# A transposed key block in the pipeline of a hybrid encoder layer: where it is transposed and copied, and how the last loads are cut

## The chip, the cores and the metric

The kernel runs on one core of a Trainium2 chip. The metric is the device time of one execution in microseconds; the median of three runs is given. A core has TensorE (PE, with its weight loads PEld), VectorE (DVE), ScalarE (ACT), GpSimd (POOL) and SyncE (SP, which here only issues DMAs). Every engine works through its own instructions in order and waits for the others by semaphores.

## What is computed

One layer over 2048 tokens of width 1024, all in float32. The reference, cut to what matters here:

```
u = rms_norm(x)
z = u @ w_in + b_in                     # q_a k_a v_a g_a lr_a | q_b k_b v_b
b = cumsum(log_sigmoid(lr_a @ w_a2 + b_a2) / 16)   # inside chunks of 64 tokens
q_dec = q_a * exp(b) / 8 ; k_inv = k_a * exp(-b) ; k_end = k_a * exp(b_last - b)
o_a = tril(q_dec @ k_inv.T) @ v_a + q_dec @ S      # gated linear attention, 4 heads
S   = exp(b_last) * S + k_end.T @ v_a              # its state, once per chunk
o_b = softmax(q_b @ k_b.T / 8 - alibi, sink) @ v_b # window of 128 tokens, 8 heads
x = x + concat(norm(o_a) * silu(g_a), o_b) @ w_out
x = x + MoE(rms_norm(x))                # 32 experts, 2 per token
y = rms_norm(x)
```

The change concerns k_end (in the code `keT`, features by tokens, and `ke`, tokens by features) and the loads of the last norm.

## The kernel before

The 2048 tokens are 16 tiles of 128. The first half of the time is the mixer: a software pipeline of steps i = 0 to 17, written by `pipeline` as two steps, a loop of seven pairs, and two steps. Step i projects tile i (`new` work), finishes attention and output of tile i-1 (`old`), and routes tile i-2 (`old2`). One function per engine (`pe_iter`, `act_iter`, `dve_iter`, `pool_iter`, `sp_iter`) writes out that engine's order by hand. Then come the routing tables, a loop over the 32 experts, and the final norm (`finish`).

`JOBS` (L91) lists what TensorE writes into PSUM in a step; entry k uses bank k mod 8, with the lag of its tile behind the step and the semaphore that tells that its result was taken. `bank_free` goes back eight entries at a time to the last job that ran in the same bank and gives the semaphore to wait for. An entry named spare is never computed and only keeps a place.

TensorE's order in step i: `qk` (queries and keys of the linear attention, transposed, 64 matmuls, L299 in the trace), `keT` (two transposes of tile i-1's decayed keys, L288), `u2Ta` and `u2Tb` (transposes of h, L288), `att` (L350), `dS` (the state's increment from `ke` and v, L361), `v` (L293), router (L376), transposes of the softmax's probabilities (L288), `g` (L293), `og`, `ob`, `kv`, `mixAT`, `qb` with the low-rank gate `la` inside (L455), a matmul for the next x (L306), `wo` in two halves (output projection, L321), and the scores `s0` to `s3` (L470).

VectorE at the end of step i: the cumulative sum and differences of the gate, `spread_x` (L642, eight products that make the next uT, for which `qk` of step i+1 waits), the first half of the routing choice (`choose`, L600 to L608), the first half of h (L780, needs the first half of `wo`), the second half of the choice (L610 to L622), the second half of h (L780), the gate's log sigmoid (L783), the three products with the decays, which make `qdkiT` and `keT` (L788, L790, L792), then the scores out of PSUM (L800, four), their maximum (L807 to L812). Step i+1 begins with the wait for the exponentials' sums, the scaling of the probabilities (L671), the bias of `qk` (L680) and `u2T` (L686, for which the router's matmuls wait).

ScalarE at the end of step i: the gates' exponentials and logarithms (L542 to L558), the three decays (L562 to L564, semaphore `decays_ready`), dec (L566), the square of h (L570, needs both halves of h), the sigmoid's exponential (L573, needs L783), eight softmax exponentials (L576) and the sink's (L577). Step i+1 then begins with the copy of the transposed keys from PSUM to `ke` (L493), for which `dS` waits.

In the final norm (`finish`) SP issues loads of h from DRAM in the pieces of `PIECES` (L1313), four loads of 1, 3, 6 and 6 tiles, and then the 16 stores of the output (L1343). ScalarE squares tile by tile (L1362), waiting for a piece at its first tile; GpSimd makes the roots in groups of three tiles (L1346, L1348), and VectorE scales (L1369). ScalarE's squares of tiles 4 on stand in its order behind two squares of the last expert's sums (L1388).

Of the kernel before, what the change touches and what calls it, by code (L numbers as in the profile page):

```python
# [75 lines left out]
class Semaphores:  # L76
# [12 lines left out]


JOBS = [  # L91
    ("qk", 0, {"qk_ready": (1, 1)}), ("keT", 1, {"ke_ready": (1, 1)}),
    ("u2Ta", 2, {"u2T_ready": (2, 1)}), ("u2Tb", 2, {"u2T_ready": (2, 2)}),
    ("att0", 1, {"att_ready": (2, 1)}), ("att1", 1, {"att_ready": (2, 2)}),
    ("dS0", 1, {"Smid_ready": (1, 1)}),
# [13 lines left out]
]  # L109
CHOOSE_STEPS = 18  # L110
INDEX = {name: k for k, (name, _, _) in enumerate(JOBS)}
# [2 lines left out]
def mixer(nc, sem, bank, A, C, scratch, ctx):  # L114
# [160 lines left out]
    def pe_iter(pe, i, par):  # L275
# [52 lines left out]
        if on("qk"):  # L328
# [3 lines left out]
            for n in range(4):  # L332
                m = project_T("qk", C_QK + n * P, C_QK + (n + 1) * P, n * P)
            m.then_inc(sem("qk_done"), 1)
        if on("keT"):
            wait(pe, sem("keT_ready"), i)
            transposes("keT", lambda c: keT[:, c * P:(c + 1) * P], 2)
        for n, name in enumerate(("u2Ta", "u2Tb")):
            if on(name):
                wait(pe, sem("h_ready"), 2 * (i - 2) + n + 1)  # L340
# [122 lines left out]
        for gg in range(2):  # L463
            if on(f"s{2 * gg}") and on(f"s{2 * gg + 1}"):
                wait(pe, sem("qbT_ready"), i + 1)
                wait(pe, sem("kb_ready"), i + 1)
                for m_ in range(2):
                    for a in range(2):
# [3 lines left out]
                        if m_ == 1:  # L472
                            m.then_inc(sem("s_done"), 1)

    BK = {name: bank[k % 8] for k, (name, _, _) in enumerate(JOBS)}


    def act_iter(act, i, par):
# [8 lines left out]
        if isinstance(i, int) and i == 0:  # L487
            square(0)
        old2 = not isinstance(i, int) or 2 <= i
        if old:  # L490
            wait(act, sem("keT_done"), i)
            wait(act, sem("dS_done"), 2 * (i - 1))
            act.activation(ke[:, :], BK["keT"][:, 0:QKA], ACT.Copy).then_inc(sem("ke_ready"), 1)  # L493
        if old2:
            wait(act, sem("router_done"), i - 1)
            wait(act, sem("router_summed"), i - 2)
# [74 lines left out]
        if new:  # L571
            wait(act, sem("lsg_ready"), i + 1)
            act.activation(g_t[:, :], g_t[:, :], ACT.Exp).then_inc(sem("sig_ready"), 1)  # L573
            wait(act, sem("nm_ready"), i + 1)
            for hh in range(HB):
                act.activation(sc[:, hh, :], sc[:, hh, :], ACT.Exp, bias=nm[:, hh:hh + 1], accum_out=sums[:, hh:hh + 1])  # L576
            act.activation(esink, esink, ACT.Exp).then_inc(sem("exps_ready"), 1)  # L577
# [46 lines left out]
    def dve_iter(v_, i, par):  # L624
# [124 lines left out]
        if new:  # L749
            wait(v_, sem("kblr_taken"), i + 1)  # L750
            wait(v_, sem("ob_done"), 2 * i)
            dve.tensor_tensor(vb[:, par, :], BK["kv"][:, P:2 * P + LOWRANK], b_tm_vb, ALU.add).then_inc(sem("vb_ready"), 1)
            if not isinstance(i, int) or i >= 1:
                dve.tensor_copy(vlo[:, :], vb[64:128, 1 - par, 0:2 * HD]).then_inc(sem("vlo_ready"), 1)

            dve.tensor_copy(kb[64:128, 0, CHUNK:], kb[0:64, 0, CHUNK:])
            dve.tensor_copy(kb[0:64, 1, CHUNK:], kb[64:128, 1, CHUNK:]).then_inc(sem("kb_ready"), 1)
            wait(v_, sem("la_ln"), i + 1)
            dve.scalar_tensor_tensor(ls[:, :], BK["la"][:, 0:QKA], 0.0, la_t[:, :], ALU.min, ALU.subtract)\
                .then_inc(sem("ls_ready"), 1)  # L760
            v_.wait_ge(sem("ls_ready"), i + 1)
            wait(v_, sem("dec_ready"), i)
            dve.tensor_tensor_scan(cum[:, :], within[:, :], ls[:, :], 0.0, ALU.mult, ALU.add).then_inc(sem("cum_ready"), 1)
            v_.wait_ge(sem("cum_ready"), 2 * i + 1)
            chunks = cum[:, :].rearrange("p (n t) -> p n t", t=CHUNK)
            dve.tensor_tensor(E[:, 1, :].rearrange("p (n t) -> p n t", t=CHUNK),
                              cum[:, CHUNK - 1::CHUNK].unsqueeze(2).to_broadcast([P, QKA // CHUNK, CHUNK]), chunks, ALU.subtract)\
                .then_inc(sem("cum_ready"), 1)
            if not isinstance(i, int) or i + 1 < NT:
                spread_x(i + 1)  # L770
        if old:
            wait(v_, sem("xr_loaded"), 16 * i)
            for n in range(2):
                if old2:
                    if n == 0:
                        wait(v_, sem("logits_ready"), i - 1)
                    choose(v_, i - 2, n)
                wait(v_, sem("wo_done"), 2 * (i - 1) + n + 1)
                hs = h[:, 1 - par, n * 512:(n + 1) * 512]
                dve.tensor_tensor(hs, BK[f"wo{n}"][:, :], hs, ALU.add).then_inc(sem("h_ready"), 1)  # L780
        if new:
            wait(v_, sem("g_ln"), i + 1)
            dve.scalar_tensor_tensor(g_t[:, :], g[:, :], 0.0, g_t[:, :], ALU.min, ALU.subtract).then_inc(sem("lsg_ready"), 1)  # L783
            wait(v_, sem("decays_ready"), i + 1)
            wait(v_, sem("og_done"), 2 * i)
            wait(v_, sem("keT_done"), i)
            qkT = qk[:, :].rearrange("p (a b) -> p a b", a=4)
            dve.scalar_tensor_tensor(qdkiT[:, 0:2, :], qkT[:, 0:2, :], DK ** -0.5, E[:, 0, :].rearrange("p (a b) -> p a b", a=2),  # L788
                                     ALU.mult, ALU.mult)
            dve.tensor_tensor(qdkiT[:, 2:4, :], qkT[:, 2:4, :], E[:, 2, :].rearrange("p (a b) -> p a b", a=2), ALU.mult)\  # L790
                .then_inc(sem("qdkiT_ready"), 1)
            dve.tensor_tensor(keT[:, :], qk[:, QKA:], E[:, 1, :], ALU.mult).then_inc(sem("keT_ready"), 1)  # L792

            wait(v_, sem("pTc1_done"), i)
            if isinstance(i, int) and i == 0:
                wait(v_, sem("late_consts"), LATE)
            for n in range(4):
                wait(v_, sem("s_done"), 4 * i + n + 1)
                heads = slice(4 * (n // 2) + n % 2, 4 * (n // 2) + 4, 2)
                dve.scalar_tensor_tensor(sc[:, heads, :], BK[f"s{n}"][:, 0:2 * WK].rearrange("p (a b) -> p a b", a=2),  # L800
                                         HD ** -0.5, alibi[:, heads, :], ALU.mult, ALU.add).then_inc(sem("s_taken"), 1)
            v_.wait_ge(sem("s_taken"), 4 * i + 4)
            if isinstance(i, int) and i == 0:
                dve.memset(C["OHcum"][:, 0, :], 0.0)
                dve.memset(sc[:, :, 0:CHUNK], NEG).then_inc(sem("filled"), 1)
                v_.wait_ge(sem("filled"), 5)
            dve.tensor_reduce(m_, sc[:, :, :], AX.X, ALU.max).then_inc(sem("softmax_steps"), 1)  # L807
            v_.wait_ge(sem("softmax_steps"), 4 * i + 1)
            dve.tensor_tensor(m_, m_, sinks[:, :], ALU.max).then_inc(sem("softmax_steps"), 1)
            v_.wait_ge(sem("softmax_steps"), 4 * i + 2)  # L810
            dve.tensor_tensor(esink, sinks[:, :], m_, ALU.subtract)
            dve.tensor_scalar(nm, m_, -1.0, None, ALU.mult).then_inc(sem("nm_ready"), 1)  # L812
# [494 lines left out]
def finish(nc, sem, bank, A, K, scratch, ctx):  # L1307
# [2 lines left out]
    def sb(name, shape, dt=F32):  # L1310
        return ctx.enter_context(nc.sbuf_tensor(name, shape, dt))

    PIECES = ((0, 1), (1, 4), (4, 10), (10, 16))  # L1313
    ROOTS = ((0, 1), (1, 4), (4, 7), (7, 10), (10, 13), (13, 16))
    Q, H = D // 4, D // 2
    hc = sb("h_back", [P, NT, D])
# [358 lines left out]
```

## Time and profile before

| | |
|---|---|
| time, median of 3 runs | 1828.28 us (1827.22 to 1830.03) |
| time of the profiled execution | 1828.53 us |
| its span, first to last instruction | 1826.5 us |
| PE / PEld busy | 1723.8 us (94%) / 1282.4 us (70%) |
| DVE / ACT / POOL busy | 581.0 (32%) / 515.0 (28%) / 276.6 us (15%) |
| mean granted TensorE clock | 0.977 of full speed |
| chain that ended last | PE 83%, DVE 7%, ACT 5%, issue 2%, DMA 2% |

Busy shares are of the span. Times of an instruction are microseconds from the span's start. In a timeline a row gives the start, the busy time, engine, line, operation, output and inputs with shapes, and a count where rows are merged; a bracket at its end gives the idle time of the engine before it and what ended that time. A chain of waits is the work that ended last, followed back from the end. Instructions of one engine overlap at their ends, so the distance of two starts is what an instruction costs in a dense row.

### The profile page before, as it was taken

The page shows a single profiled execution, that of the slowest core. Times are in us where ns is not written, and L with a number is a line of the kernel's source. Part 1 is how long each engine was busy: PE and PEld are TensorE (multiplying, and loading weights), DVE is VectorE, ACT ScalarE, POOL GpSimd, SP SyncE. Part 2 cuts the span into 40 slices and gives each one's busy share as a digit, 9 for nine tenths or more (in the row PEclk, how much of TensorE's full clock was granted, in tenths as well). Part 3 has the DMA queues.
Part 4 walks back from the last instruction along what each step waited for, and adds up shares of the span by engine and source line. Part 5 has one row for each costly group of instructions (what it writes and reads, how often), then busy time and mean ns, then how long its engine had stood idle before and what let it go on. Part 6 is the DMA issues. An engine that isn't in the chain of part 4 may idle for free.

```text
span 1826.5 us, 30836 instructions
## 1 busy us (share of the span) xinstructions
PE 1723.8 (94%) x11328; PEld 1282.4 (70%) x11329; DVE 581.0 (32%) x1558; ACT 515.0 (28%) x1319; POOL 276.6 (15%) x344
## 2 busy tenths in 40 slices
PE   6899999999999999999975999999999999999990
PEld 5577676776767666676644788878888887878880
DVE  1343435534455334453446111111111111111114
ACT  1434424344244442444424111111111111111113
POOL 0001010110101101010010122211222222222132
PEclk9899999999999999999987999999999999999995
DMA  9411011110111101101123889989999899999998
GB/s 350 108 53 42 24 58 57 46 46 23 57 57 46 42 27 57 57 34 42 38 76 130 279 271 337 296 301 312 337 319 325 268 336 309 317 320 315 311 296 339
DMA packets 130499, 322.34 MB, mean 176 GB/s; under 512 B 10712, under 2 KB 18921, under 8 KB 130468
## 3 DMA queue, kind: packets, MB, share of 16 engines
q1 hardware_dynamic: 113956, 278.71, 43.4%
q0 software_dynamic: 15648, 43.11, 9.2%
q8 instruction: 20, 0.33, 0.1%
q10 hardware_dynamic: 864, 0.10, 0.0%
q14 instruction: 11, 0.09, 0.0%
HBM read 274.86 MB, written 47.19 MB: 176 GB/s over the span
## 4 chain that ended last, share of the span: by engine, by line
PE 83%; DVE 7%; ACT 5%; issue 2%; DMA 2%; POOL 0%; DVEq 0%; ACTq 0%; POOLq 0%; SPq 0%
PE bank L293 14%; PE bank L1185 13%; PE bank L1196 13%; PE bank L321 12%; PE bank L1221 12%; PE bank L299 9%; ACT sc L576 3%; PE bank L1153 2%; PE bank L288 2%; DVE sc L800 2%; DVE sm L807 2%; PE bank L1210 1%; PE bank L959 1%; PE bank L376 1%; PE bank L419 1%
## 5 line engine op out<-in xcount | busy, mean ns | idle before, releaser
L299 PE MATMUL bank<-uT,w_in_sb 128*128 128x128 f32 x2304 | 277.0, 279 | 3.3 <-DVE uT L642 3.3
L299 PEld LDWEIGHTS bank<-uT,w_in_sb 128*128 128x128 f32 x2304 | 266.3, 194 | 15.5 <-issue 13.3
L1185 PEld LDWEIGHTS bank<-xT,wts 128*128 128x128 f32 x2048 | 248.7, 191 | 23.3 <-issue 19.1
L293 PE MATMUL bank<-w_in_sb,uT 128*128 128x512 f32 (+1 forms) x768 | 264.1, 497 | 0.0
L1185 PE MATMUL bank<-xT,wts 128*128 128x128 f32 (+2 forms) x2048 | 252.9, 283 | 4.6 <-issue 3.6
L1196 PE MATMUL bank<-xT,wts 128*128 128x128 f32 (+2 forms) x2048 | 247.9, 282 | 0.0
L1196 PEld LDWEIGHTS bank<-xT,wts 128*128 128x128 f32 x2048 | 245.0, 191 | 0.0
L1221 PE MATMUL bank<-wts,hT 128*128 128x512 f32 x512 | 231.8, 595 | 0.0
L321 PE MATMUL bank<-w_out_sb,mixT 128*128 128x512 f32 x512 | 222.7, 593 | 1.5 <-ACT mixT L520 0.8
L293 PEld LDWEIGHTS bank<-w_in_sb,uT 128*128 128x128 f32 x768 | 128.0, 191 | 112.0 <-issue 112.0
L1276 DVE TENSOR_TENSOR hT<-bank,sg 128x160 f32<-128x160 f32 x128 | 41.5, 325 | 442.2 <-PE bank L1196 442.2
L321 PEld LDWEIGHTS bank<-w_out_sb,mixT 128*128 128x128 f32 x512 | 96.0, 190 | 116.5 <-issue 114.3
L1221 PEld LDWEIGHTS bank<-wts,hT 128*128 128x128 f32 x512 | 92.2, 190 | 97.6 <-issue 97.6
L823 POOL TENSOR_SCALAR ss<-ss 128x1 f32<-128x1 f32 (+1 forms) x49 | 11.3, 231 | 830.9 <-ACT junk L570 428.9
L1242 ACT ACTIVATE y<-bank,gatec 128x256 f32<-128x256 f32 x31 | 14.7, 473 | 333.6 <-PE bank L1221 187.5
L1104 POOL DMA_INDIRECT h_dram<-y,putc x62 | 99.0, 1597 | 34.8 <-POOL putc L1111 25.3
L1111 POOL COPY putc<-put 128x2 int32 (+1 forms) x31 | 5.7, 183 | 519.7 <-DVE y L1284 519.7
L1231 ACT ACT_TABLE_LOAD x31 | 39.8, 1283 | 152.7 <-PE bank L1185 152.7
L576 ACT ACTIVATE sc<-sc,sm 128x192 f32<-128x192 f32 x128 | 56.3, 441 | 66.3 <-DVE sm L812 66.3
L1231 ACT ACTIVATE sg<-bank 128x160 f32<-128x160 f32 x128 | 38.8, 303 | 122.7 <-PE bank L1185 122.4
L1257 DVE TENSOR_TENSOR xT<-bank,norm_sb 128x128 f32<-128x128 f32 x66 | 16.1, 286 | 115.5 <-PE bank L1153 115.5
L1284 DVE TENSOR_SCALAR y<-bank,gatec 128x512 f32<-128x512 f32 x31 | 23.3, 751 | 91.4 <-PE bank L1221 91.4
(243 smaller groups left out, 1687.7 us busy)
## 6 DMA issues: line engine op xcount, KB each, us to landing
wts<-w_gate_in SPq DMA_DIRECT2D x32, 2048.0 KB, 11.1
wts<-w_up_in SPq DMA_DIRECT2D x32, 2048.0 KB, 9.4
wts<-w_down_in SPq DMA_DIRECT2D x32, 2048.0 KB, 9.3
x_sb<-x_in SPq DMA_DIRECT2D x17, 512.0 KB, 3.6
xT_in<-x_t_in SPq DMA_DIRECT2D x17, 512.0 KB, 4.5
w_in_sb<-w_in_in SPq DMA_DIRECT2D x4, 2048.0 KB, 12.1
h_sb<-x_in SPq DMA_DIRECT2D x16, 512.0 KB, 3.3
h_dram<-h_sb SPq DMA_DIRECT2D x16, 512.0 KB, 2.9
```

The lines of the kernel that those rows point to most:

```text
L288: m = pe.transpose(bk[name][:, c * P:(c + 1) * P], src(c), ident)
L293: m = pe.matmul(bk[name][:, col:col + hi - lo], uT[:, k, :], w_in[:, k, lo:hi], start=k == 0, stop=k == KD - 1)
L299: m = pe.matmul(bk[name][0:hi - lo, col:col + P], w_in[:, k, lo:hi], uT[:, k, :], start=k == 0, stop=k == KD - 1)
L321: m = pe.matmul(bk[f"wo{n}"][:, :], mixT[:, k, :], w_out[:, k, n * 512:(n + 1) * 512], start=k == HA, stop=k == HA - 1)
L576: act.activation(sc[:, hh, :], sc[:, hh, :], ACT.Exp, bias=nm[:, hh:hh + 1], accum_out=sums[:, hh:hh + 1])
L800: dve.scalar_tensor_tensor(sc[:, heads, :], BK[f"s{n}"][:, 0:2 * WK].rearrange("p (a b) -> p a b", a=2), HD ** -0.5, alibi[:, heads, :], A ...
L1104: po.indirect_dma_start(out=table, out_offset=bass.IndirectOffsetOnAxis(ap=putc[:, col:col + 1], axis=0), in_=src, in_offset=None, compute ...
L1185: m = pe.matmul(G[m_ % 2][:, 0:w], wg[:, k, m_ * P:(m_ + 1) * P], xT[:, k, 0:w], start=k == 0, stop=k == KD - 1)
L1196: m = pe.matmul(U[m_ % 2][:, 0:w], wu[:, k, m_ * P:(m_ + 1) * P], xT[:, k, 0:w], start=k == 0, stop=k == KD - 1)
L1221: m = pe.matmul(YB[half][:, :], hT[:, k, 0:P], wd[:, k, half * 512:(half + 1) * 512], start=k == 0, stop=k == KF - 1)
L1231: act.activation(sg[:, m_, 0:n_], G[m_ % 2][:, 0:n_], ACT.Silu).then_inc(sem(pre + "sg_ready"), 1)
L1276: nc.vector.tensor_tensor(hT[:, m_, 0:n_], U[m_ % 2][:, 0:n_], sg[:, m_, 0:n_], ALU.mult)\
```

## The change

`keT` moves in three engines' orders, and two loads are cut in two.

- TensorE: the two transposes `keT` of tile i move from behind `qk` of step i+1 to the end of step i, behind the scores. In `JOBS` `keT` gets the last place (bank 7 in place of 1) with lag 0, and a spare takes its old place with the semaphore of h's second half.
- VectorE: the three products with the decays move from behind the gate's log sigmoid to the place directly behind `spread_x`, ahead of the routing choice and both halves of h.
- ScalarE: the copy to `ke` moves from the head of step i+1 to step i, between the sigmoid's exponential and the softmax's exponentials.
- The final norm's loads are 1, 3, 3, 3, 3 and 3 tiles.

```diff
@@ JOBS
-    ("qk", 0, {"qk_ready": (1, 1)}), ("keT", 1, {"ke_ready": (1, 1)}),
+    ("qk", 0, {"qk_ready": (1, 1)}), ("spare1", 2, {"h_ready": (2, 2)}),
...
-    ("spare0", -1, {"uT_ready": (2, 2)}), ("spare1", -1, {"uT_ready": (2, 2)}),
+    ("spare0", -1, {"uT_ready": (2, 2)}), ("keT", 0, {"ke_ready": (1, 1)}),
@@ pe_iter, behind qk
-        if on("keT"):
-            wait(pe, sem("keT_ready"), i)
-            transposes("keT", lambda c: keT[:, c * P:(c + 1) * P], 2)
@@ pe_iter, behind the scores s0 to s3
+        if on("keT"):
+            wait(pe, sem("keT_ready"), i + 1)
+            transposes("keT", lambda c: keT[:, c * P:(c + 1) * P], 2)
@@ act_iter, head of the step
-        if old:
-            wait(act, sem("keT_done"), i)
-            wait(act, sem("dS_done"), 2 * (i - 1))
-            act.activation(ke[:, :], BK["keT"][:, 0:QKA], ACT.Copy).then_inc(sem("ke_ready"), 1)
@@ act_iter, behind the exponential of g_t
+            wait(act, sem("keT_done"), i + 1)
+            wait(act, sem("dS_done"), 2 * i)
+            act.activation(ke[:, :], BK["keT"][:, 0:QKA], ACT.Copy).then_inc(sem("ke_ready"), 1)
+
             wait(act, sem("nm_ready"), i + 1)
@@ dve_iter, behind spread_x(i + 1); the same lines go behind the log sigmoid (L783)
+            wait(v_, sem("decays_ready"), i + 1)
+            wait(v_, sem("og_done"), 2 * i)
+            wait(v_, sem("keT_done"), i)
+            qkT = qk[:, :].rearrange("p (a b) -> p a b", a=4)
+            dve.scalar_tensor_tensor(qdkiT[:, 0:2, :], qkT[:, 0:2, :], DK ** -0.5, E[:, 0, :].rearrange("p (a b) -> p a b", a=2),
+                                     ALU.mult, ALU.mult)
+            dve.tensor_tensor(qdkiT[:, 2:4, :], qkT[:, 2:4, :], E[:, 2, :].rearrange("p (a b) -> p a b", a=2), ALU.mult)\
+                .then_inc(sem("qdkiT_ready"), 1)
+            dve.tensor_tensor(keT[:, :], qk[:, QKA:], E[:, 1, :], ALU.mult).then_inc(sem("keT_ready"), 1)
@@ finish
-    PIECES = ((0, 1), (1, 4), (4, 10), (10, 16))
+    PIECES = ((0, 1), (1, 4), (4, 7), (7, 10), (10, 13), (13, 16))
```

## Rows read from the trace of the kernel before

**Rows 1.** The page: its first line.
```profile
span 1826.5 us, 30836 instructions
```

**Rows 2.** Waits of PE: who waited for whom, us in total, times, longest.
```profile
PE bank L361 <- ACT ke L493: 15.9, 16, 6.0
```

**Rows 3.** Stretch of one step: length; busy PE, PEld, DVE, ACT, POOL; clock; DMA share, GB/s.
```profile
518.75:576.18 57.43, 57.13 (x365) 38.93 (x365) 25.55 (x73) 22.46 (x60) 5.33 (x8) 1.00 0.12 46
```

**Rows 4.** Chain of waits, where `wo` ends in steps 1 and 15.
```profile
116.74 0.02 issue
...
920.74 0.02 issue
```

**Rows 5.** Timeline of PE over the border of two middle steps.
```profile
518.66 1.57 PE L470 MATMUL bank<-kb_sb,qbT 64*128 64x192 f32 x16
...
527.41 0.38 PE L288 MATMUL bank<-ident,keT 128*128 128x128 f32 x2
...
528.60 0.46 PE L350 MATMUL bank<-qdkiT 64*64 64x64 f32 x16
529.36 0.67 PE L361 MATMUL bank<-v_sb,ke 64*64 64x128 f32 x16 [0.30 <-ACT ke L493]
...
537.02 1.07 PE L376 MATMUL bank<-u2T,w_r_sb 128*36 128x128 f32 x16
```

**Rows 6.** Timeline of ACT over the same border.
```profile
512.84 0.40 ACT L564 ACTIVATE decays<-decays 128x256 f32<-128x256 f32 x1
...
525.23 0.45 ACT L576 ACTIVATE sc<-sc,sm 128x192 f32<-128x192 f32 x1 [4.07 <-DVE sm L812]
...
528.85 0.36 ACT L493 ACTIVATE ke<-bank 128x256 f32<-128x256 f32 x1
```

**Rows 7.** Timeline of DVE over the same border.
```profile
507.03 2.15 DVE L642 SCALAR_TENSOR_TENSOR uT<-xT_in,norm_sb,bank 128x128 f32<-128x128 f32 x8
...
511.98 0.69 DVE L780 TENSOR_TENSOR h_sb<-bank,h_sb 128x512 f32<-128x512 f32 x1 [0.89 <-PE bank L321]
...
518.77 0.69 DVE L780 TENSOR_TENSOR h_sb<-bank,h_sb 128x512 f32<-128x512 f32 x1 [3.48 <-PE bank L321]
519.38 0.68 DVE L783 SCALAR_TENSOR_TENSOR g_t<-g_sb,g_t 128x512 f32<-128x512 f32 x1
519.98 0.42 DVE L788 SCALAR_TENSOR_TENSOR qdkiT<-qk_sb,decays 128x256 f32<-128x256 f32 x1
...
520.98 1.94 DVE L800 SCALAR_TENSOR_TENSOR sc<-bank,alibi 128x384 f32<-128x384 f32 x4
...
531.90 1.27 DVE L686 TENSOR_TENSOR u2T<-bank,norm_sb 128x512 f32<-128x512 f32 x2
```

**Rows 8.** Timeline of PE from step 0 into step 1.
```profile
54.81 7.38 PE L299 MATMUL bank<-uT,w_in_sb 128*128 128x128 f32 x64 [1.00 <-DVE uT L642]
...
68.83 1.13 PE L361 MATMUL bank<-v_sb,ke 64*64 64x128 f32 x16 [6.03 <-ACT ke L493]
```

**Rows 9.** Timeline of ACT in step 0: the last of its three decays.
```profile
58.32 0.40 ACT L564 ACTIVATE decays<-decays 128x256 f32<-128x256 f32 x1
```

**Rows 10.** Chain of waits: `v` of step 1.
```profile
69.96 9.65 PE bank L293 x16
```

**Rows 11.** Stretches of 1 us in steps 1 and 16: columns as in rows 3.
```profile
75.00:76.00 1.00, 1.00 (x3) 0.38 (x2) 0.00 (x0) 0.00 (x0) 0.00 (x0) 0.93 0.00 0
...
938.00:939.00 1.00, 1.00 (x8) 1.00 (x7) 0.00 (x0) 0.74 (x2) 0.00 (x0) 0.65 0.03 12
```

**Rows 12.** Timeline of PE in step 16: the router's matmuls.
```profile
934.58 1.93 PE L376 MATMUL bank<-u2T,w_r_sb 128*36 128x128 f32 x16 [2.10 <-DVE u2T L686]
```

**Rows 13.** Final norm: the four loads of L1340, and issue to landing.
```profile
L1340 SPq DMA_DIRECT2D h_back<-h_dram x4: 357/544/715, 1772.7 to 1774.3; - x4
...
DMA to landing us min/median/max: 3.7/13.4/24.0
```

**Rows 14.** Timeline of ACT in the final norm: the square of tile 10.
```profile
1799.81 1.04 ACT L1362 ACTIVATE fjunk<-h_back 128x1024 bf16<-128x1024 f32 x1
```

More of the change, by code:

```diff
@@ L783, in dve_iter @@
             dve.scalar_tensor_tensor(g_t[:, :], g[:, :], 0.0, g_t[:, :], ALU.min, ALU.subtract).then_inc(sem("lsg_ready"), 1)
[L784 to L792, printed above, removed]
             wait(v_, sem("pTc1_done"), i)
```

## The prediction, made before the changed kernel was run

> **What bounds the kernel now.** I read the page first: PE is busy 94% of the span of 1826.5 us and makes 83% of the chain that ended last [rows 1]. So a step's length is PE's own work plus what PE waits for, and the view that prices this change is that of PE's waits. The reader is to see there that PE waited 15.9 us in 16 times for the copy to `ke` (L493), of which one took 6.0 us [rows 2]. Then the stretch of one middle step: 57.43 us with 57.13 us of PE, at full clock [rows 3]; the idle 0.30 us is the one in front of `dS` [rows 5]. From the end of `wo` in step 1 to that in step 15 are 920.74 - 116.74 = 804.0 us, 14 times 57.43 [rows 4], so all these steps are alike. The timelines say why PE waits: the copy (528.85) stands behind nine exponentials that begin at 525.23 [rows 6], and these hang on the scores, which VectorE takes at 520.98 [rows 7].
>
> **The middle steps.** On ScalarE the copy now stands in front of the exponentials. `keT` must be there for it. On VectorE: `decays_ready` comes at 512.84 + 0.40 = 513.24 [rows 6]. The three products take 520.98 - 519.98 = 1.00 us [rows 7], so `keT` is ready near 514.3. PE arrives behind its scores at 518.66 + 1.50 = 520.2 [rows 5] and doesn't wait; the transposes end near 520.5. The copy's next predecessors on ScalarE are the square of h and the sigmoid's exponential, some 1.9 us behind h and the log sigmoid: from about 520.3 they end near 522.2, the copy ends near 522.6, 2.6 us ahead of the exponentials (525.23). `dS` is reached by PE at 528.60 + 0.46 = 529.06 and finds it 6 us old. Gain 0.30 us a step; PE's own work is the same number of matmuls in another order.
>
> What is late next? The wait for the decays stands ahead of both halves of h on VectorE. Before, choice 1 began at 507.03 + 2.07 = 509.10 and ended 0.89 us ahead of 511.98, at 511.09: 1.99 us; choice 2 ran from 511.98 + 0.61 to 518.77 - 3.48 = 515.29: 2.70 us [rows 7]. Now: products 513.27 to 514.27, choice 1 to 516.26, first half of h to 516.87, choice 2 to 519.57, second half of h (its matmuls end at 518.75) to 520.18, log sigmoid to 520.78, then the scores: 0.20 us earlier than the 520.98 of before. The 3.5 us in which VectorE waited for `wo` pay for it. The first half of h comes 4.3 us later; `qk` of the next step needs its bank at 520.5, 3.6 us later. The second comes 0.8 us later; `u2T`'s transposes need it at 527.6. SP's store of h goes out 0.8 us later, and `h_stored` is needed only behind `u2T` (from 531.90), over 10 us on; GpSimd's root of the second norm and its gate product move by the same 0.8 us, again against users at 529 and later. The router, the nearest waiter behind the softmax, comes at 537.02 and its operand is done at 531.90 + 1.27 = 533.17: 3.8 us of slack. So nothing new binds, and I take 14 x 0.30 = **-4.2 us** (bounds: 0, if a hidden cost of issue replaces the wait, and -4.4).
>
> **The first border.** Here `keT` is not early. In step 0 the decays end at 58.32 + 0.40 = 58.72 [rows 9], `keT` near 59.85, so PE, done with its scores at 53.81, waits until 60.0 with `qk` of step 1 queued behind the transposes, where before `qk` began at 54.81 [rows 8]. The wait of 6.03 us in front of `dS` goes instead. Before, the cold clock (half, 1.2 GHz) after that wait made `dS` 1.13 instead of 0.67 us and `v` 9.65 instead of 7.06 us (in a middle step from 529.96, where `dS` ends, to 537.02), 3.05 us in all [rows 5, 8, 10]; it rose at 75.07, 6.2 us after work began again at 68.83 [rows 11]. A wait of 6.2 us should do the same to `qk`. From 53.81 to the end of `v`: before 79.62 - 53.81 = 25.8 us; after 6.2 (wait) + 0.3 + 7.2 (qk) + 0.5 (att) + 0.6 + 7.0 + 3.05 (cold) = 24.9 us. I take **-0.9** (bounds +0.5 and -2.3, with the clock staying low for 3 us less or more). The scores and softmax shift by 0.6 us, as the log sigmoid now stands behind the products, and their users are at 79.
>
> **The last border.** The third long wait (5.7 us, what is left of 15.9) gives nothing: in step 16 the router waits for `u2T`, which stands on VectorE behind the softmax [rows 12]. `dS` only runs earlier into idle time. The scores' 0.2 us lead remains: -0.2. But the clock rose there at 938.65 [rows 11], 7.3 us after `dS` began and 4.1 us after the router began at 934.58; with `dS` moved away from it, the low clock may last up to 2 us longer, which costs half of that. I take **+0.3** for both (bounds -0.8 and +0.8).
>
> **The last loads.** They are issued from 1772.7 to 1774.3 and the last lands 24.0 us after its issue, at 1798.3 [rows 13]. ScalarE reaches the first tile of that piece, 10, at 1799.81 with no idle time [rows 14], the square of tile 4 already behind two squares of VectorE's sums. So loads in smaller pieces are early for someone who isn't waiting. The two more issues on SP cost 2 x 0.54 = 1.1 us ahead of stores that begin at 1781. The first two pieces, for which ScalarE does wait, keep their size and place. **0** (bounds +0.4 for two more waits on ScalarE, and -0.5).
>
> Sum: -4.2 - 0.9 + 0.3 + 0 = **-4.8 us**. The profiled execution took 1828.53 us; 1823.7 follows for it, and as it lies 0.25 us above the median of 1828.28, 1823.5 for a median. The bounds of the middle steps lie further on the side of a smaller gain, so I forecast **1823.8 us**.
>
> **Rivals.**
>
> (a) *The edges take it back.* The low clock lasts longer at both borders (+1.4 and +0.5 against my values), and the routing's matmuls, which run partly cold, meet the rise later by 1 us. Then -4.8 + 1.4 + 0.5 + 0.5 = -2.4: about 1825.9 us. For it: where the clock rises differs from 4.1 to 7.3 us behind the start of work. Against: it can as well come sooner.
>
> (b) *The wait hid PE's issue.* `dS` is 16 short matmuls behind 16 short ones of `att` and 10 transposes; while PE stood, its sequencer could fill the queue. Without the wait `dS` and the start of `v` could be held up by issue for about the same 0.25 us. Then the 14 steps give only 14 x 0.05 = 0.7 and the sum is -1.3: 1827.1 us. Against it: `att`, in the same place, runs 16 matmuls in 0.46 us without a wait ahead of it [rows 5]. The Trainium skill speaks for this rival (TensorE: Matmul & The Clock Gate, "Wait — 56ns, not 53.3ns?"): with hardware decode off the sequencer spends about 62 ns on a matmul, and this bounds short ones; by it `dS` would need about 16 x 62 = 1.0 us instead of 0.6, an estimate from that page, and the steps would gain nothing. The 29 ns of a matmul in `att` disagree unless they were queued ahead.
>
> (c) *VectorE becomes the bound: slower than before.* Everything behind the decays on VectorE, h and the scores with it, now hangs on ScalarE's gate chain. It decides when `u2T` ends over 3.8 us later than now, that is, when the decays come later than 513.24 + 0.20 + 3.8 = 517.3. Price: each us beyond is a us of PE in each of 14 steps; the decays at 517.8, say, cost 0.5 - 0.3 = 0.2 net a step, +2.8, and with 518.0 +5.6: 1833 us. Against: ScalarE's chain to the decays depends on `la` alone, not on anything that moved.
>
> (d) *More than the sum*: the clock at the first border rises 3 us sooner (-1.4 more) and the loads' landing shortens the final norm by 1 us: 1821.4 us. Nothing waits for the cut loads, so this is little more than luck.
>
> The Trainium skill (DMA: Bandwidth & Descriptors, "Anatomy of one DMA") gives each DMA a fixed cost of about 2 us, mostly completion. If two more DMAs paid that one after another, an estimate by that page, the last piece would land at 1802.3; tile 13 would be squared from 1802.9, so even then nobody waits. No row here shows a fixed cost apart from the transfer.
>
> **Chances.** Forecast 0.55, with its own range 1822.4 to 1825.0; (a) 0.20, (b) 0.12, (c) 0.05, (d) 0.08. The range 1820.9 to 1827.4 us holds the forecast, (a), (b)'s better half and (d). A measurement of this kernel can tell about 0.2%, 3.7 us, from no change: faster means below 1824.6. From the forecast 0.48 of its 0.55 lie below, from (a) 0.04 and (d) all: 0.60 faster. (c) gives 0.05 slower, and 0.35 is left for the same.
>
> **What would show it.** Right: PE's waits no longer name L493; a middle step is 57.13 us long; the scores (L800) begin 0.2 us earlier against the end of `wo`, and the copy to `ke` ends over 2 us ahead of the exponentials; between step 0's scores and the transposes of `keT` PE stands about 6 us and `qk` of step 1 takes about 10 us; the router of step 16 still waits for `u2T`; ScalarE's squares of tiles 4 to 15 come at the same distance from the first store. Wrong: idle time marked as issue in front of `dS` or `v` (b), an idle PE in front of L376 in middle steps (c), or a final norm, from the first load to the end, that differs by over 0.5 us.

## The result, and the profile after

The changed kernel takes 1820.38 us (median of 6 runs, 1819.26 to 1821.98) against 1829.46 us of the kernel before (6 runs, 1827.22 to 1830.76): ratio 0.995, 95% interval 0.9939 to 0.996, 9.1 us less. The forecast was 1823.8 with a range down to 1820.9: the sign was right, and the gain about twice the 4.8 us of the sum. The profiled execution took 1820.15 us, 8.4 less than that of before.

The page of the changed kernel: its span, the busy times, and the engines' shares of the chain that ended last. PE's share of that chain was 83% and is 90%, VectorE's went from 7% to 2% and ScalarE's from 5% to 2%: the middle steps' part of the chain no longer runs over the scores, the exponentials and the copy.

```profile
span 1818.0 us, 30847 instructions
...
PE 1718.6 (95%) x11328; PEld 1281.1 (70%) x11329; DVE 586.2 (32%) x1558; ACT 515.6 (28%) x1319; POOL 274.8 (15%) x344
...
PE 90%; DMA 2%; DVE 2%; ACT 2%; issue 2%; POOL 1%; DVEq 0%; ACTq 0%; POOLq 0%; SPq 0%
```

Waits of TensorE after: who waited for whom, us in total, times, longest. The 16 waits for `ke` [rows 2] are gone. The long wait of step 16 stands in front of the router, and one of 6.2 us for `keT` is new.

```profile
PE bank L373 <- DVE u2T L687: 9.6, 2, 8.8
...
PE bank L288 <- DVE keT L780: 6.2, 1, 6.2
```

One middle step after, as in [rows 3] (length, then busy PE, PEld, DVE, ACT, POOL, clock): 56.87 us where it was 57.43, with no idle PE. Under it the border inside (PE, as in [rows 5]).

```profile
511.25:568.12 56.87, 56.87 (x365) 38.78 (x365) 25.89 (x74) 22.49 (x60) 5.20 (x8) 1.00 0.12 46
```

```profile
511.17 1.57 PE L467 MATMUL bank<-kb_sb,qbT 64*128 64x192 f32 x16
512.68 0.44 PE L288 MATMUL bank<-ident,keT 128*128 128x128 f32 x2
...
521.06 0.46 PE L347 MATMUL bank<-qdkiT 64*64 64x64 f32 x16
521.35 0.62 PE L358 MATMUL bank<-v_sb,ke 64*64 64x128 f32 x16
521.90 7.13 PE L293 MATMUL bank<-w_in_sb,uT 128*128 128x512 f32 x16
528.97 1.07 PE L373 MATMUL bank<-u2T,w_r_sb 128*36 128x128 f32 x16
```

ScalarE and VectorE at the same border, as in [rows 6, 7]. `keT` ends at 506.9; the copy starts at 514.37 and ends at 514.73, 3.1 us ahead of the exponentials; the scores start 2.10 us behind PE's first scores, where they started 520.98 - 518.66 = 2.32 behind.

```profile
514.37 0.36 ACT L573 ACTIVATE ke<-bank 128x256 f32<-128x256 f32 x1
517.84 0.46 ACT L577 ACTIVATE sc<-sc,sm 128x192 f32<-128x192 f32 x1 [3.11 <-DVE sm L812]
```

```profile
506.47 0.42 DVE L780 TENSOR_TENSOR keT<-qk_sb,decays 128x256 f32<-128x256 f32 x1
...
513.27 1.95 DVE L800 SCALAR_TENSOR_TENSOR sc<-bank,alibi 128x384 f32<-128x384 f32 x4
```

TensorE from step 0 into step 1, as in [rows 8]: the stop is now in front of `keT`, and `qk`, not `v`, runs on the low clock.

```profile
51.08 1.57 PE L467 MATMUL bank<-kb_sb,qbT 64*128 64x192 f32 x16 [1.68 <-ACT qbT L546]
58.84 0.66 PE L288 MATMUL bank<-ident,keT 128*128 128x128 f32 x2 [6.19 <-DVE keT L780]
59.30 8.87 PE L299 MATMUL bank<-uT,w_in_sb 128*128 128x128 f32 x64
...
68.38 0.62 PE L358 MATMUL bank<-v_sb,ke 64*64 64x128 f32 x16
68.94 1.55 PE L293 MATMUL bank<-w_in_sb,uT 128*128 128x512 f32 x3
```

The clock in stretches of 1 us (the column behind POOL's), as in [rows 11]: half until 62.6 (0.72 in the stretch that follows 62), 3.7 us after work began at 58.84; in step 16 until 926.1 (0.93 in the stretch that follows 926).

```profile
62.00:63.00 1.00, 1.00 (x9) 1.00 (x8) 1.00 (x1) 0.00 (x0) 0.73 (x1) 0.72 0.96 311
925.00:926.00 1.00, 1.00 (x7) 0.93 (x6) 0.96 (x4) 0.55 (x2) 0.00 (x0) 0.50 0.91 356
926.00:927.00 1.00, 1.00 (x11) 1.00 (x9) 0.17 (x1) 0.78 (x2) 0.00 (x0) 0.93 0.05 21
```

Step 16 and the final norm after, as in [rows 12 to 14]: `dS` runs early, the router waits for `u2T` as before, and tile 10 is squared 1791.23 - 1764.0 = 27.2 us behind the first load (before 1799.81 - 1772.7 = 27.1).

```profile
913.78 0.67 PE L358 MATMUL bank<-v_sb,ke 64*64 64x128 f32 x16
923.21 1.93 PE L373 MATMUL bank<-u2T,w_r_sb 128*36 128x128 f32 x16 [8.76 <-DVE u2T L687]
```

```profile
L1340 SPq DMA_DIRECT2D h_back<-h_dram x6: 357/630/4435, 1764.0 to 1767.3; - x6
...
DMA to landing us min/median/max: 10.1/15.8/22.3
```

```profile
1791.23 1.04 ACT L1362 ACTIVATE fjunk<-h_back 128x1024 bf16<-128x1024 f32 x1
```

Laid side by side, the profiles of before, after and of most of the experiments below give this table. Times are us between starts of PE's rows. "Placing" is the first group of the routing's placing matmuls (L959, 64 at once), "end" the end of the span; the fifth column runs from the scores of step 0 to placing.

| kernel | scores of step 0 to 1 | one middle step (mean of 14) | scores of step 15 to placing | sum of these | placing to end |
|---|---|---|---|---|---|
| before | 64.42 | 57.43 | 59.28 | 927.70 | 846.6 |
| loads in pieces only | 63.74 | 57.43 | 58.92 | 926.72 | 848.4 |
| changed kernel | 62.03 | 56.87 | 58.74 | 916.90 | 850.0 |
| changed, loads as before | 62.07 | 56.87 | 58.76 | 916.96 | 849.8 |
| before, copy moved alone | 56.44 | 56.92 | 60.02 | 913.27 | 846.9 |
| changed, copy put back | 62.08 | 57.55 | 58.79 | 926.61 | 848.1 |
| changed, copy put back in 8 pieces | 62.47 | 57.93 | 59.83 | 933.36 | 846.5 |
| changed, `u2T` first in step 16 | 62.48 | 56.87 | 57.48 | 916.09 | 849.6 |
| copy moved alone, `u2T` first | 56.44 | 56.91 | 57.67 | 910.87 | 850.3 |
| changed, step 0 in the old order, `u2T` first | 56.41 | 56.87 | 57.91 | 910.54 | 848.9 |

Down to the placing matmuls the change gains 927.2 (mean of the first two rows) - 916.9 = 10.3 us: 2.0 at the first border, 14 x 0.56 = 7.9 in the middle steps, 0.4 in step 16. Behind it the code is the same, yet that stretch differs by 4 us among these kernels, and by 6 with the kernels of twelve added matmuls below (852.2 and 852.8). In it the two placing groups alone, which start behind waits of 8.0 and 2.4 us, take 18.4 to 20.8 us by when the clock comes back, and the first 64 matmuls of the kernel (`qk` of step 0) take 8.7 to 10.3 us. This goes to no part of the change: the kernels with TensorE's old order have 846.6 to 852.8 us there, those with the new one 846.5 to 852.2.

### The profile page after: what moved, and what is told of

It is laid out like the page before. It is cut to its first block, busy times and chain, and to the rows that moved or that the text cites. A ratio compares the mean times of both kernels' runs of the same rounds, so it can differ in the third digit from the quotient of the medians.

```text
span 1818.0 us, 30847 instructions
## 1 busy us (share of the span) xinstructions
PE 1718.6 (95%) x11328; PEld 1281.1 (70%) x11329; DVE 586.2 (32%) x1558; ACT 515.6 (28%) x1319; POOL 274.8 (15%) x344
## 4 chain that ended last, share of the span: by engine, by line
PE 90%; DMA 2%; DVE 2%; ACT 2%; issue 2%; POOL 1%; DVEq 0%; ACTq 0%; POOLq 0%; SPq 0%
PE bank L299 14%; PE bank L293 14%; PE bank L1185 12%; PE bank L1196 12%; PE bank L1221 12%; PE bank L321 11%; PE bank L288 3%; PE bank L1153 2%; PE bank L1210 1%; PE bank L467 1%; PE bank L959 1%; PE bank L373 1%; DMA xg<-v_dram,idxc 1%; PE bank L416 1%; PE bank L397 1%
```

## The experiments

**Which part of the change does it.** Two kernels split the loads from the rest.

```diff
@@ kernel before, loads in pieces only
-    PIECES = ((0, 1), (1, 4), (4, 10), (10, 16))
+    PIECES = ((0, 1), (1, 4), (4, 7), (7, 10), (10, 13), (13, 16))
@@ changed kernel, loads as before
-    PIECES = ((0, 1), (1, 4), (4, 7), (7, 10), (10, 13), (13, 16))
+    PIECES = ((0, 1), (1, 4), (4, 10), (10, 16))
```

> The kernel before with only the last loads cut into pieces of three tiles. Theory (nothing waits for the cut loads): time ratio 1.000 to the kernel before, within 1 us; span from the first load's issue to the end 53.8 us as before (1772.7 to 1826.5). Rival (the loads' landing or SP's issue matters): the stretch from the first load's issue to the end changes by over 0.5 us. The changed kernel's 54.0 us (1764.0 to 1818.0) speaks for no gain.

> The changed kernel with the last loads as before. Theory: all of the change's 9 us lie in the mixer, so this is as fast as the changed kernel, 1820.4 us (0.995). Rival: the pieces carry part of it, and this one is 1 us or more slower than that. Middle step 56.87 us in both cases.

Measured: 1829.61 us against 1829.08 for the pieces alone (ratio 1.0001, 0.9992 to 1.001), and 1820.27 (0.995, 0.9934 to 0.9965) for the move alone. The whole gain is the move's; the pieces are worth nothing, as forecast.

**Which engine's part of the move does it.** In the kernel before, only ScalarE's copy moves; PE and VectorE keep their orders. The reverse: the changed kernel with the copy put back behind the exponentials.

```diff
@@ kernel before, act_iter: the three lines leave the head of the step
-            act.activation(ke[:, :], BK["keT"][:, 0:QKA], ACT.Copy).then_inc(sem("ke_ready"), 1)
...
+            wait(act, sem("keT_done"), i + 1)
+            wait(act, sem("dS_done"), 2 * i)
+            act.activation(ke[:, :], BK["keT"][:, 0:QKA], ACT.Copy).then_inc(sem("ke_ready"), 1)
             wait(act, sem("nm_ready"), i + 1)
@@ changed kernel, copy put back
-            act.activation(ke[:, :], BK["keT"][:, 0:QKA], ACT.Copy).then_inc(sem("ke_ready"), 1)
...
             act.activation(esink, esink, ACT.Exp).then_inc(sem("exps_ready"), 1)
+            wait(act, sem("keT_done"), i + 1)
+            wait(act, sem("dS_done"), 2 * i)
+            act.activation(ke[:, :], BK["keT"][:, 0:QKA], ACT.Copy).then_inc(sem("ke_ready"), 1)
```

> The kernel before with nothing moved but ScalarE's copy to ke, which goes ahead of the softmax's exponentials of the step; TensorE and VectorE keep their order. The exponentials now wait for the transposes behind qk: from 525.2 to about 528.2 in a middle step, so u2T ends near 536.1 against a router that PE would reach at 536.5. Theory A (a wait in front of dS costs PE 0.17 us more than the idle time that the trace shows, as the matmuls' ends are modelled, so that 0.56 us a step go with the wait wherever keT is transposed): middle step 56.9 us, -7.5 us. Theory B (the extra 0.26 us of the changed kernel come from the new place of the transposes): middle step 57.13 us, -4.2 us. In both, at the first border PE doesn't stand for keT (6.2 us in the changed kernel) and its clock stays up, so v of step 1 ends 7 to 9 us earlier than before; total -12 to -17 us, near 1814 us. If the exponentials' 2.9 us delay does bind, PE idles in front of L376 and the step is 57 us or more.

> The changed kernel with ScalarE's copy to ke back behind the exponentials (PE and VectorE in the new order). It ends near 0.45 us behind the time at which PE could begin dS. Theory A (a stop of PE costs what its successor is really late, some 0.2 us more than the shown idle time): middle step 57.3 to 57.45 us, idle shown 0.2 to 0.35 us. Theory B (the new place of the transposes saves 0.26 us by itself): middle step about 57.1 us. Total against before: A 0 to -2 us in the middle steps, B -4; at the first border the copy ends behind the exponentials at about the time PE is through with qk, so little changes there.

Measured: the copy alone 1814.64 us (0.9908, 0.9893 to 0.9922), 5.7 us faster than the changed kernel in medians, and its middle step of 56.92 us is the one of theory A: the gain goes with the wait, wherever `keT` is transposed. With the copy put back 1828.57 us (0.9997, 0.9989 to 1.0006): nothing is left of the gain. PE and its waits in the kernel with the copy alone, from step 0 into step 1:

```profile
52.67 1.57 PE L470 MATMUL bank<-kb_sb,qbT 64*128 64x192 f32 x16 [1.68 <-ACT qbT L545]
...
62.77 0.46 PE L350 MATMUL bank<-qdkiT 64*64 64x64 f32 x16
63.41 0.67 PE L361 MATMUL bank<-v_sb,ke 64*64 64x128 f32 x16 [0.17 <-ACT ke L572]
64.00 7.13 PE L293 MATMUL bank<-w_in_sb,uT 128*128 128x512 f32 x16
```

In step 0 the transposes of `keT` are done at 62.9 and the exponentials begin at 65.15, so a copy in front of them no longer waits for them to end. The long stop is gone: `dS` starts 0.17 us late and `v` runs at full clock, so this border costs 56.44 us, 5.6 less than in the changed kernel, where PE stands 6.2 us for `keT` before it can do `qk`. In a middle step ScalarE waits in front of the copy until PE has done `qk` and the transposes, and the exponentials start 9.45 us behind the scores instead of 6.57; `u2T` is done 0.46 us ahead of the router (3.8 before), which just suffices. These steps take 56.92 us against 56.87. Step 16 is 0.9 us longer than before, the clock coming back 5.7 us behind the router's start. In sum 7.6 + 7.2 - 0.9 = 13.9 us. So the move on ScalarE is the gain, and the move on PE and VectorE adds 0.05 us a step (0.7 in all) and costs 5.6 at the start. With the copy put back, the wait in the middle steps is 0.50 to 0.54 us (the first of the 14 has none) and the step 57.55 us, both above theory A's ranges. PE reaches `att` 0.05 us sooner behind the scores than before and the copy starts up to 0.08 us later; the rest is that `dS` starts 0.26 us behind the copy's end (525.84 + 0.36) instead of 0.15 ([rows 5, 6]), which no run here explains. These steps give back 1.7 of the 2.0 us of the first border:

```profile
525.84 0.36 ACT L577 ACTIVATE ke<-bank 128x256 f32<-128x256 f32 x1
```

```profile
525.46 0.46 PE L347 MATMUL bank<-qdkiT 64*64 64x64 f32 x16
526.46 0.67 PE L358 MATMUL bank<-v_sb,ke 64*64 64x128 f32 x16 [0.53 <-ACT ke L577]
```

```profile
PE bank L358 <- ACT ke L577: 12.8, 14, 6.1
```

**How much a shown wait costs.** The 0.30 us of idle time [rows 5] were worth over 0.5. In this kernel the copy put back is cut into eight pieces of 32 columns, which lengthens the wait.

```diff
@@ changed kernel, copy behind the exponentials and in eight pieces
-            act.activation(ke[:, :], BK["keT"][:, 0:QKA], ACT.Copy).then_inc(sem("ke_ready"), 1)
+            for c in range(8):
+                m = act.activation(ke[:, 32 * c:32 * c + 32], BK["keT"][:, 32 * c:32 * c + 32], ACT.Copy)
+            m.then_inc(sem("ke_ready"), 1)
```

> The changed kernel with the copy to ke behind the exponentials and made in eight pieces of 32 columns, so that it ends some 0.4 to 0.9 us later still. Theory A (the shown idle time in front of dS understates the stop by a fixed 0.19 us, as in the two kernels measured so far: shown 0.30 and 0.53, start of att to start of dS 0.76 and 1.00 against 0.28 without a stop): the step is 57.02 us plus the shown idle time, and att to dS is 0.47 us plus it. Rival (the understatement grows with the wait, so that the trace would miss a share of it): the difference is over 0.25 us here.

Measured in a single execution: 1833.99 us beside 1830.18 of the kernel before, a middle step 57.93 us. PE in it, and the waits:

```profile
529.51 0.46 PE L347 MATMUL bank<-qdkiT 64*64 64x64 f32 x16
530.87 0.67 PE L358 MATMUL bank<-v_sb,ke 64*64 64x128 f32 x16 [0.90 <-ACT ke L578]
```

```profile
PE bank L358 <- ACT ke L578: 18.2, 14, 6.5
```

From the start of `att` to that of `dS`: 0.29 us in the changed kernel without a wait; 0.76 before with 0.30 shown [rows 5]; 1.00 with 0.53; 1.36 with 0.90; at the first border with the copy moved alone 0.64 with 0.17. Less the undisturbed 0.285, these stops cost 0.475, 0.715, 1.075 and 0.355: each 0.18 us more than its idle time shows, for idle times from 0.17 to 0.90 us. The group of `att` in the trace of before says why:

```profile
L350 PE MATMUL bank<-qdkiT x256: 218/218/268, 62.3 to 925.4; 64*64 64x64 f32 x128
```

One of these matmuls is given 218 ns from start to end, but 16 start within 0.29 us, 18 ns apart. In the profile, whose ends of matmuls are modelled, a matmul that doesn't wait starts inside the end of the one ahead; one that waits starts behind it, and the overlap of 0.218 - 0.018 = 0.20 us is lost with the wait and stands in the busy time (by the rows, 0.46 us busy less the 0.285 that the group costs without a wait, 0.18). The Trainium skill (TensorE: Matmul & The Clock Gate, "Single matmul latency") puts a lone warm bf16 matmul of the full array at (398 + N) / 2.4 ns, by an estimate from it 192 ns for N = 64, and most of it drain. The row's 218 ns, for 64x64 matmuls in float32, are near it.

**The low clock at the first border.** Twelve matmuls of 5.45 us in all (24 in the trace, two for each), whose results nobody reads, fill the stop: in step 0 of the changed kernel in front of `keT`, in step 1 of the kernel before in front of `dS`. A first pair had 24 of them.

```diff
@@ changed kernel, pe_iter, in front of keT (24 in the first pair)
+            if isinstance(i, int) and i == 0:
+                for _ in range(12):
+                    pe.matmul(bk["keT"][:, 2 * P:4 * P], ident, w_in[:, 0, 0:2 * P], start=True, stop=True)
@@ kernel before, pe_iter, in front of dS (24 in the first pair)
+        if isinstance(i, int) and i == 1:
+            for s_, n_ in bank_free(INDEX["dS0"], 1):
+                wait(pe, s_, n_)
+            for _ in range(12):
+                pe.matmul(bk["dS0"][:, 2 * P:4 * P], ident, w_in[:, 0, 0:2 * P], start=True, stop=True)
```

> The changed kernel, with 24 matmuls added in step 0 whose results are never read (ident by 256 columns of w_in, written beside keT in its bank); TensorE runs them while it would stand 6.2 us for keT. They touch nothing of the wait itself. Theory (the first border came out better than forecast because the low clock after such a wait lasted only about 3.9 us, and costs about half of that): the clock stays at full, qk of step 1 takes 7.4 us instead of 8.9, and the border from the scores of step 0 to those of step 1 becomes 62.05 - 1.5 = 60.5 us; the time falls by about 1.5 us, to 1818.9. Rival (qk of step 1 is slow for another reason, the loads of weights that still run then): qk stays at 8.9 us at full clock and the border at 62.0.

> The kernel before, with 24 matmuls added in step 1 whose results are never read (ident by 256 columns of w_in, into columns of a dS bank that nobody uses); TensorE runs them while it stands 6.0 us for the copy to ke in front of dS. Theory: the low clock after that wait cost 3.05 us there (dS 1.13 instead of 0.67, v 9.65 instead of 7.06). With the clock kept at full, dS takes 0.67 and v 7.1 us and the border from the scores of step 0 to those of step 1 becomes 64.1 - 3.05 = 61.1 us; the time falls by 3.0 us, to about 1826. The changed kernel's border, 62.05, then differs from the one of before only in how long the low clock lasts and not in what waits. Rival (the order itself saves the 2 us at this border): the border stays above 63 us although the clock is full.

With 24 the matmuls took 10.63 us and outlasted the stop, so both kernels came out slower than expected: 1826.01 us (0.9984, 0.9975 to 0.9994) and 1832.68 (1.002, 1.0011 to 1.003). What followed the stop ran at full clock in both.

> As the run with 24 added matmuls in step 0, with 12: each of the 24 took 0.443 us (10.63 us in all) and so they outlasted the wait by over 4 us; 12 take 5.3 of its 6.2 us. Theory: the clock stays full across the wait. In the run with 24, from the start of keT's transposes in step 0 to the scores of step 1 were 117.19 - 64.72 = 52.47 us; in the changed kernel they were 113.11 - 58.84 = 54.27. With 12 the wait ends where it did, so the border from scores to scores becomes 62.03 - 1.80 = 60.2 us and the time falls by 1.8 us against the changed kernel's ratio of 0.995 to before: 0.994, about 1818.6. Rival (that stretch was shorter only because 4 us more had passed for the loads and the softmax): qk of step 1 takes 8.9 us, border 62.0, time 1820.4.

> As the run with 24 added matmuls in step 1 of the kernel before, with 12: 5.3 us of the 6.0 that TensorE stands in front of dS. Theory: with 24, from the start of dS in step 1 to the scores of step 1 were 117.14 - 72.37 = 44.77 us, against 116.66 - 68.83 = 47.83 in the kernel before. With 12 the wait ends where it did, so the border from scores to scores becomes 64.42 - 3.06 = 61.4 us, and the time falls by 3 us: ratio 0.998. Rival (that stretch was shorter only because 4 us more had passed for the loads and ScalarE): dS and v stay at 1.13 and 9.65 us, ratio 1.000.

PE with 12 in the changed kernel, its clock in the stretch from 60 to 61 us, and PE with 12 in the kernel before:

```profile
51.97 1.57 PE L467 MATMUL bank<-kb_sb,qbT 64*128 64x192 f32 x16 [1.68 <-ACT qbT L549]
54.45 5.45 PE L475 MATMUL bank<-w_in_sb,ident 128*128 128x256 f32 x24 [0.91 <-DVE uT L646]
...
59.95 7.31 PE L299 MATMUL bank<-uT,w_in_sb 128*128 128x128 f32 x64
...
112.20 1.57 PE L467 MATMUL bank<-kb_sb,qbT 64*128 64x192 f32 x16
```

```profile
60.00:61.00 1.00, 1.00 (x12) 1.00 (x11) 1.00 (x3) 0.79 (x2) 0.01 (x1) 1.00 0.97 311
```

```profile
52.03 1.57 PE L475 MATMUL bank<-kb_sb,qbT 64*128 64x192 f32 x16 [1.67 <-ACT qbT L554]
...
62.52 5.45 PE L359 MATMUL bank<-w_in_sb,ident 128*128 128x256 f32 x24
68.63 0.67 PE L366 MATMUL bank<-v_sb,ke 64*64 64x128 f32 x16 [0.66 <-ACT ke L498]
...
113.40 1.57 PE L475 MATMUL bank<-kb_sb,qbT 64*128 64x192 f32 x16
```

The borders take 112.20 - 51.97 = 60.23 and 113.40 - 52.03 = 61.37 us, as expected (60.2 and 61.4): the low clock costs 1.80 us in the changed kernel and 3.05 in the one before. Of the 2.39 us between the two profiles' borders 1.25 are thus the clock's, which came back 3.7 us behind the start of work instead of 6.3 [rows 11], and 1.14 the order's. The clock's part is that of these two executions: behind the same stop in the kernel with the loads in pieces alone the clock came back after 4.9 us, and in four other kernels with the changed kernel's stop after 3.3 to 4.7. The whole times: 1820.21 us (0.9941, 0.9928 to 0.9955) where 0.994 was expected, an interval that holds the changed kernel's 0.995 too, and 1829.4 (0.9997, 0.9987 to 1.0006) where 0.998 was, which the interval leaves out. In the second case's profiled execution the 3 us are lost behind the placing: 852.8 us to the end against 846.6 before. Of these 6.2 us the two placing groups take 2.3 (10.32 and 10.41 us against 9.16 and 9.22), and the experts, from the first to the last of their matmuls with `xT`, 3.6 (774.5 against 770.9). The changed kernel with 12 spends 4.5 us more in the experts too (776.2 against 771.7) and makes up half of it in the placing groups, so neither total shows the border alone. PE's waits named issue in the experts' first matmuls show most of it, in the kernel before and in the changed one with 12 (the one before with 12 has 6.6 us in 4):

```profile
PE bank L1185 <- issue: 3.6, 2, 1.9
```

```profile
PE bank L1188 <- issue: 6.7, 4, 2.1
```

Why identical code stops four times instead of twice, some 2 us each, these runs don't say.

**The last border.** The router of step 16 waits 8.8 us for `u2T`, which on VectorE stands behind the wait for the exponentials' sums. For that step alone (i == NT) its two products, `scale_u2T` in the diff, go ahead of that wait, in the changed kernel and in the one with the copy moved alone; a third kernel is the changed one with `u2T` first in step 16 and step 0 in the old order (`keT` behind `qk` of step 1, the products behind the log sigmoid).

```diff
@@ dve_iter, step 16, ahead of the wait for exps_ready
+        if isinstance(i, int) and i == NT:
+            scale_u2T()
...
+            if not (isinstance(i, int) and i == NT):
+                scale_u2T()
@@ pe_iter, third kernel
-        if on("keT"):
+        if not (isinstance(i, int) and i == 0) and on("keT"):
...
+        if isinstance(i, int) and i == 1:
+            for s_, n_ in bank_free(INDEX["keT"], 0):
+                wait(pe, s_, n_)
+            wait(pe, sem("keT_ready"), 1)
+            transposes("keT", lambda c: keT[:, c * P:(c + 1) * P], 2)
```

> The changed kernel with one move in step 16 alone: VectorE scales u2T ahead of its wait for the exponentials' sums, so the router's matmuls run inside the softmax and PE's next work waits for the probabilities. Theory: the wait in front of the router (8.8 us in the changed kernel) and 1.9 us of router matmuls at the low clock leave the path; the transposes of the probabilities begin about 3 us earlier (near 922 in place of 925), the sum of og waits a little for the state: -2.5 us against the changed kernel, 1818 us. Rival: PE's next stop (attm, S on VectorE behind the probabilities) takes it all, or the low clock lasts longer: under 1 us.

> The kernel before with ScalarE's copy to ke ahead of the exponentials and u2T ahead of the wait in step 16: the two edits add, as they act at different places: 1814.5 - 2.5 = 1812 us (ratio to before 0.9905 - 0.0014 = 0.989). If not, the last border is bound by something both share.

> The changed kernel, but in the first border in the old order (keT of tile 0 behind qk of step 1, the log sigmoid ahead of the products in step 0), and with u2T ahead of the wait in step 16. Theory: PE never stands for keT (6.2 us) nor for the copy (6.0 us), its clock stays up; the first border costs what it costs with the copy alone moved (56.4 us from scores to scores against 62.0 of the changed kernel), the middle steps are 56.87 us (0.045 less than with the copy alone moved). So 0.6 us less than the kernel with copy and u2T moved: near 1811.5 us. Rival: the low clock at the border has another cause than PE's stop, then the border stays near 60 us.

Measured: 1817.6 us (0.9929, 0.9915 to 0.9942), 1813.31 (0.9909, 0.9894 to 0.9924) and 1811.08 (0.9895, 0.988 to 0.9911). Waits and PE of the first of them in step 16:

```profile
PE bank L373 <- DVE u2T L667: 3.7, 2, 2.8
PE bank L288 <- DVE sc L682: 2.8, 1, 2.8
```

```profile
918.93 1.93 PE L373 MATMUL bank<-u2T,w_r_sb 128*36 128x128 f32 x16 [2.81 <-DVE u2T L667]
923.68 1.09 PE L288 MATMUL bank<-ident,g_t 128*128 128x128 f32 x4 [2.82 <-DVE sc L682]
```

```profile
928.00:929.00 1.00, 1.00 (x20) 0.86 (x19) 0.00 (x0) 0.00 (x0) 0.00 (x0) 0.84 0.00 0
```

The router starts 8.02 us behind the scores instead of 13.97, but the transposes of the probabilities still wait for the softmax, 12.77 us behind the scores instead of 15.83, and the clock, back 17.4 us behind the scores (at 928.3) instead of 16.9 (at 926.1), takes over half of that away: 57.48 us for the step where the changed kernel has 58.74. So the -2.5 us that were expected are 1.3 at this border in this pair of profiles, though the medians differ by 2.8. In the copy-alone pair the border gives 2.4 (60.02 and 57.67), but the medians differ by 1.3 and the ratio is 0.9909 where 0.989 was expected; the stretch behind the placing is 3.4 us longer there. What the edit is worth stays open between 1.3 and 2.4 us. The third kernel, 1811.08 us where 1811.5 was expected, is the fastest of all, 9.3 us below the changed one by the medians and 19 below the kernel before.

## Why the prediction was wrong, step by step

**The middle steps** (forecast -4.2, measured -7.9). The mechanism held: the wait is gone, the copy is done over 3 us early (2.6 forecast), the scores come 0.22 us earlier (0.20), nothing new waits. The size failed: "Gain 0.30 us a step". The stop cost 0.475 and not 0.30, as its row shows idle time only. The group of `dS` behind it took 0.60 us from start to start where it takes 0.55 without a wait (521.35 to 521.90), and 0.05 us are gained in the head of the step, where `keT` now runs between the scores and `qk`. The kernel with the copy alone bears this out: it keeps the old head and gains 0.51 us a step. The bound of -4.4 that I gave was therefore none. The forecast of a step of 57.13 us, busy PE alone, failed with it: busy PE fell too, to 56.87.

**The first border** (forecast -0.9, measured -2.39 by the two profiles, -2.0 against the mean of the unchanged borders). The stop of "6.0 us" came as forecast, 6.19. The order gave 1.14 for my 0.9; 0.2 of that is the same error, as the sum has 0.5 for `att`, which costs 0.28 where nothing waits (68.10 to 68.38). The step "a wait of 6.2 us should do the same to `qk`", 3.05 us, failed: it was 1.80. My bound of -2.3 allowed for the clock, though not for the -2.39 of the two profiles. The rise of the clock in [rows 11] was also misread: 0.93 of a stretch that is half low until the rise puts it at 75.14 and not 75.07, 6.3 us behind the start of work, and 0.65 at 938.7 and not 938.65; neither moves the sum.

**The last border** (forecast +0.3, measured -0.2 to -0.5). The router waits for `u2T` and starts 13.97 us behind the scores (13.92 before), so the 0.2 us lead went nowhere; the clock came back 2.9 us behind the router's start and not later than the 4.1 of before. In the twelve-matmul kernel the same code took 59.90 us where the changed one took 58.74: this term is chance.

**The last loads** (forecast 0). Right: 1.0001, final norm 54.0 us against 53.8. The fixed 2 us that the prediction took from the Trainium skill (DMA: Bandwidth & Descriptors, "Anatomy of one DMA") stand there for DMAs that GpSimd issues; these are SP's, and no run here shows such a cost.

The terms as measured are -7.9 - 2.0 - 0.4 = -10.3. The medians have 9.1; the 1.2 us between are put down to no part, as the start of the kernel and the second half vary by more than that with the clock and the issue stops. Rival (a) is out, since neither edge took anything back; the routing's placing groups did take 20.6 us in the changed kernel's profile against 18.4, but with the loads in pieces alone, in the old order, they took 20.8. Rival (b) is out: `att` and `dS` without a wait run 16 matmuls in 0.29 and 0.55 us. By an estimate from the 62 ns a matmul that the Trainium skill (TensorE: Matmul & The Clock Gate, "Wait — 56ns, not 53.3ns?") gives for hardware decode off, each would take about 1.0 us; the rows disagree with it. Rival (c) is out: the decays arrive at 505.8, h isn't waited for. Rival (d) had the sign of the surprise at the first border, not its main source. What I never asked is which of the moves the gain needs: the copy alone, leaving PE's order as it was, gives 14.4 us.

## What to carry to other kernels

Price a stop of TensorE by the distance of two starts against the same distance where nothing waits, or add to the idle time shown the length of the last matmul less the spacing of its group; in a loop the difference is paid in every turn. When a move touches three engines, ask for each engine alone what it gains: a transfer to the steady state's best order can cost the pipeline's first step more than it saves in all the others. A stop that is avoided where the work behind it is dense is worth its length and what the low clock takes afterwards; one that is only filled gives back the clock's part alone (1.80 and 3.05 us here).

## What the runs showed of the hardware

The two placing groups, 64 matmuls each of unchanged code, take 9.16 and 9.22 us in one profile and 10.22 and 10.36 in another; `qk` of step 0 takes 8.7 to 10.3. How long the low clock lasts behind a stop of some 6 us was not repeatable from kernel to kernel: 6.3 and 4.9 us behind the same stop of 6.0 us in the kernel before and the one with the loads in pieces alone, 3.3 to 4.7 us behind the changed kernel's stop of 6.2 us. It cost 3.05 us where it lasted 6.3 and 1.80 where it lasted 3.7. Twelve matmuls whose results nobody reads kept it from falling at all in the two kernels that had them.
